# Recurrence levels kept as running products of the forget gates in a hybrid attention and recurrence decoder step

## The reference, cut to what matters

```
f = lb + (1 - lb) * sigmoid(fr);  q = silu(qr);  k = 1 - f;  v = ir
S_t = diag(f_t) S_{t-1} + k_t v_t^T          o_t = S_t^T q_t
# chunkwise: b = cumsum(log f) inside a chunk
scores[t, s] = sum_k q[t, k] * k[s, k] * exp(b[t, k] - b[s, k])   for s <= t
o = scores @ v + (q * exp(b)) @ S0
S = exp(b_last) * S0 + (k * exp(b_last - b))^T v
```

## Time and profile before

| | |
|---|---|
| time, median of 3 runs | 2099.07 us (2098.29 to 2101.21) |
| the profiled execution | 2095.78 us, of which the span of instructions is 2093.6 us |
| busy, share of the span | PE 95%, PEld 90%, DVE 57%, ACT 36%, POOL 37% |
| mean granted TensorE clock | 0.976 |
| the interleaved stage, layer 0 | 402.9 us (first `qk`) to 541.75 us (first `att_unit`) |
| the same, layer 1 | 1430.2 us to 1571.3 us |

### The profile page before, as it was taken

The page is one execution under the profiler, slowest core; times in us unless marked ns, Lnnn a source line. Parts: engine busy times, 40 slices in busy tenths (PEclk is TensorE's granted clock), DMA queues, the critical chain, the costliest instruction groups (busy, mean ns, idle before and its releaser), DMA issues.

```text
span 2093.6 us, 40399 instructions
## 1 busy us (share of the span) xinstructions
PE 1991.8 (95%) x15746; PEld 1890.4 (90%) x15746; DVE 1183.2 (57%) x2150; ACT 746.7 (36%) x1139; POOL 784.6 (37%) x452
## 2 busy tenths in 40 slices
PE   6999999988999999999999999998899999999998
PEld 6988999866799999999998889997678999999998
DVE  4577788676456442154337787886754654413531
ACT  4343232455233342222423442234632343322222
POOL 2632357210144443433465223651102434444342
PEclk9999999899899999999999999998998999999999
DMA  6232245202333232332342323541033332233322
GB/s 165 86 92 71 64 120 169 85 2 83 113 95 88 85 87 83 101 89 72 90 142 64 82 62 81 149 132 55 1 107 108 107 91 85 77 90 101 90 67 85
DMA packets 310129, 189.20 MB, mean 90 GB/s; under 512 B 15993, under 2 KB 295769, under 8 KB 308977
## 3 DMA queue, kind: packets, MB, share of 16 engines
q1 hardware_dynamic: 300368, 160.51, 27.1%
q0 software_dynamic: 4224, 16.78, 2.4%
q10 hardware_dynamic: 5408, 10.16, 1.4%
HBM read 167.47 MB, written 18.10 MB: 89 GB/s over the span
## 4 chain that ended last, share of the span: by engine, by line
PE 80%; DVE 7%; issue 4%; ACT 3%; POOL 3%; DMA 1%; PEld 0%; SPq 0%; DVEq 0%; PEldq 0%; POOLq 0%; ACTq 0%
PE acc L859 64%; PE work L1253 3%; PE work L820 2%; POOL w_lo L690 2%; PE work L1195 1%; PE work L998 1%; POOL k_sel L756 1%; DVE std L1973 1%; PE acc L1163 1%; PE work L885 1%; PE work L1288 1%; PE work L1063 1%; PE work L1101 1%; DVE mix L2621 1%; ACT w_hi L1461 1%
## 5 line engine op out<-in xcount | busy, mean ns | idle before, releaser
L690 POOL TENSOR_TENSOR w_lo<-raw,w_hi 128x1024 fp32r<-128x1024 f32 (+3 forms) x290 | 623.1, 2149 | 971.6 <-ACT w_hi L1461 967.0
L859 PE MATMUL acc<-normed,w_hi 128*128 128x268 f32 x5696 | 957.8, 290 | 3.3 <-POOL w_lo L690 1.6
L859 PEld LDWEIGHTS acc<-normed,w_hi 128*128 128x128 f32 x5696 | 801.8, 190 | 26.8 <-issue 20.0
L1461 ACT ACTIVATE w_hi<-raw 128x1024 fp32r<-128x1024 f32 (+1 forms) x286 | 289.1, 1011 | 936.6 <-PE acc L859 936.6
L859 PE MATMUL acc<-normed,w_lo 128*128 128x268 f32 x2848 | 585.0, 287 | 0.0
L859 PEld LDWEIGHTS acc<-normed,w_lo 128*128 128x128 f32 x2848 | 445.5, 189 | 0.0
L859 PE MATMUL acc<-hidden,w_hi 128*128 128x268 f32 x1408 | 231.5, 286 | 0.0
L859 PEld LDWEIGHTS acc<-hidden,w_hi 128*128 128x128 f32 x1408 | 197.0, 188 | 0.0
L859 PE MATMUL acc<-hidden,w_lo 128*128 128x268 f32 x704 | 144.2, 286 | 0.0
L2658 DVE TENSOR_TENSOR hidden<-act_f,hidden 128x536 f32 x44 | 93.3, 2121 | 50.6 <-ACT hidden L1871 50.6
L2651 DVE TENSOR_TENSOR silu<-silu,rnorm 128x536 f32<-128x536 f32 x44 | 83.4, 1895 | 59.1 <-ACT silu L1868 59.1
(11 more groups left out here) (346 smaller groups left out, 2801.2 us busy)
## 6 DMA issues: line engine op xcount, KB each, us to landing
raw<-in_w_in_dram SPq DMA_DIRECT2D x90, 512.0 KB, 3.9
raw<-in_w_gu_dram SPq DMA_DIRECT2D x88, 512.0 KB, 3.8
raw<-in_w_down_dram SPq DMA_DIRECT2D x32, 384.0 KB, 3.4
raw<-in_w_down_dram SPq DMA_DIRECT2D x32, 320.0 KB, 3.1
gate_scratch<-gate_out ACTq DMA_DIRECT2D x32, 268.0 KB, 3.0
normed<-gate_scratch SPq DMA_DIRECT2D x4, 2144.0 KB, 9.4
raw<-in_w_o_dram SPq DMA_DIRECT2D x16, 512.0 KB, 4.1
raw<-in_w_pa_dram SPq DMA_DIRECT2D x16, 256.0 KB, 3.4
```

What stands on the lines that cost most here:

```text
L690: pool.tensor_tensor(w_lo[s][:, 0:kt, :], raw[slot][:, 0:kt, :], w_hi[s][:, 0:kt, :].bitcast(f32), ALU.subtract).then_inc(lo_done, 1)
L859: mm = pe.matmul(acc[o][:, half, 0:HT], w[s][:, k, :], mov[:, part, k0 + k, half * HT:(half + 1) * HT], start=start and n == 0, stop=stop ...
L1461: act.activation(w_hi[slot % 2][:, 0:kt, :], raw[slot][:, 0:kt, :], ACT.Copy).then_inc(hi_done, 1)
```

## The change

- The logarithm, the scans, the differences, all exponentials of the recurrence and `X0` to `X2` go. q is multiplied once with f into a new buffer `XQ` (`spread(0, hp)`); k stays in `K`.
- The levels run from span 1 up to span 64, `level(i, h)`, for one head at a time, in the two 512-column halves of `work[1]` by turns. Between two levels `spread(i, hp)` multiplies, in place, the queries of each later half with the product of the gates over the earlier half, and the keys of each earlier half with that over the later one. After the seventh spread `XQ` and `K` are what the chunk steps need.
- POOL makes the products over 2, 4, ... 128 tokens in a chain of seven multiplications and a copy (`totals`, `last_decay`), ahead of the two `rest`s that stood at the stage's beginning.
- Score masks are copied for one head at a time: 28 copies of 512 columns' half in place of 14 of twice that, and four for the diagonal in place of two.
- One level per step in steps 2 to 8, chunks in steps 9 to 13, 18 steps in all. Blocks 2 and 3 change places. `qk` of block 2 stands behind the turning of the sample tokens instead of ahead.
- `s0` has memory of its own, so the first two state loads start at the stage's beginning; all four heads' sample work lies within the stage, `rank1(3)` ahead of block 15, and nothing of it between the `att_unit`s. `gate_return(0)` starts behind the turned keys of the tail.

```diff
+    SPANS = [1, 2, 4, 8, 16, 32, 64]
+    BLK = [(0, 0), (0, 1), (0, 4), (0, 2)] + [(n2, j) for j in range(3) for n2 in range(1, 4)] + [(n2, 3) for n2 in range(4)]
+    SAMPLE_OF = {11: 0, 13: 1, 15: 2, 16: 3}
+    PE_AHEAD = {1: [("diagonal", 0), ("diagonal", 1)]}
+    PE_AMID = {1: [("diagonal", 2), ("diagonal", 3)]}
+    PE_BEHIND = {1: [("v_turn", 3), ("v_turn", 4)], 2: [("level_tail", 0), ("level_tail", 1)]}
+    DVE_AHEAD = {0: ["keys"], 1: [("diagonal", 0), ("diagonal", 1)]}
+    DVE_BEHIND = {0: [("spread", 0, 0), ("spread", 0, 1)], 1: [("diagonal", 2), ("diagonal", 3)]}
+    for i in range(7):
+        tail = [("level_tail", i + 1)] if 1 <= i <= 3 else []
+        PE_AHEAD[i + 2] = [("level", i, 0), ("level", i, 1)] + tail
+        PE_AMID[i + 2] = [("level", i, 2), ("level", i, 3)]
+        DVE_AHEAD[i + 2] = [("scores", i, 0), ("scores", i, 1)] + ([("spread", i + 1, 0)] if i else [])
+        DVE_BEHIND[i + 2] = [("scores", i, 2), ("scores", i, 3)] + ([("spread", i + 1, 1), ("tail", i + 1)] if 1 <= i <= 3 else
+                                                                   [("spread", i + 1, 1)] if i else
+                                                                   [("tail", 0), ("tail", 1), ("spread", 1, 0), ("spread", 1, 1)])
+    for c in range(5):
+        PE_AMID[9 + c] = [("decayed", c)]
+        PE_BEHIND[9 + c] = [("rec_out", c), ("state", c)]
+        ACT_AHEAD[10 + c] = [("rec_out", c)]
+        DVE_AHEAD[10 + c] = [("state", c)]
...
+                for i, span in enumerate((2, 4, 8, 16, 32, 64, 128)):
+                    n = (TP if span <= 16 else 512) // span
+                    if i:
+                        wait(pool, "span_total", L, 8, i)
+                    of = (totals[i - 1] if i else B[:, 4:8, :])[:, :, 0:2 * n].rearrange("p h (b e) -> p h b e", e=2)
+                    to = totals[i][:, :, :] if i < 6 else last_decay[:, :, 0:4]
+                    pool.tensor_tensor(to, of[:, :, :, 0], of[:, :, :, 1], ALU.mult).then_inc(S["span_total"], 1)
...
-                        for h in range(4):
-                            wait(act, "forget", L, 4, h + 1)
-                            act.activation(log_f[:, h, :], B[:, 4 + h, 0:TP], ACT.Ln).then_inc(S["log_forget"], 1)
...
+                def spread(i, hp):
+                    at = slice(2 * hp, 2 * hp + 2)
+                    if i == 0:
+                        TT(XQ[:, at, :], B[:, at, 0:TP], B[:, 4 + 2 * hp:6 + 2 * hp, 0:TP], ALU.mult)\
+                            .then_inc(S["lev_ready"], 1)
+                        return
+                    span = SPANS[i - 1]
+                    w = TP if span <= 8 else 512
+                    n = w // (2 * span)
+                    if i == 1:
+                        wait_rec_filled(vec, L, ("diagonal", 2 * hp + 1))
+                        wait(vec, "tail_filled", L, 5, 2)
+                    elif i <= 4:
+                        wait(vec, "tail_filled", L, 5, i + 1)
+                    if i >= 2:
+                        wait(vec, "span_total", L, 8, i - 1)
+                    wait_rec_filled(vec, L, ("level", i - 1, 2 * hp + 1))
+                    hold(vec)
...
+                    TT(q, q, of[:, :, :, 0:1].broadcast_to((P, 2, n, span)), ALU.mult).then_inc(S["lev_ready"], 1)
+                    TT(k, k, of[:, :, :, 1:2].broadcast_to((P, 2, n, span)), ALU.mult).then_inc(S["lev_ready"], 1)
...
-                att_unit(0)
-                late_sample(2)
-                att_unit(1)
-                rank1(3)
-                att_unit(2)
-                late_sample(3)
-                att_unit(3)
+                for n in range(4):
+                    att_unit(n)
```

More of the change, by code:

```diff
@@ L1244, in diagonal @@
                                        start=True, stop=True)
-                    rec_finish(mm, ("diagonal", hp))
-                def level(lev, hp):
-                    ps, at = rec_begin(("level", lev, hp)), X[lev % 3]
-                    wait(pe, "lev_ready", L, 14, 2 * lev + 2)
-                    for m in range(8):
-                        h, c = 2 * hp + m // 4, m % 4
-                        mm = pe.matmul(ps[:, m * P:(m + 1) * P], at[:, h, c * P:(c + 1) * P], at[:, h, c * P:(c + 1) * P],
-                                       start=True, stop=True)
-                    rec_finish(mm, ("level", lev, hp))
@@ L1257, in level_tail, with level @@
-                def level_tail(lev):
-                    m = TAILS.index(lev)
-                    if m:
-                        wait(pe, "tail_drained", L, 5, m)
-                    left, right = (K, B) if lev == 7 else (X[lev % 3], X[lev % 3])
+                    rec_finish(mm, ("diagonal", h))
+                def level(i, h):
+                    ps = rec_begin(("level", i, h))
+                    wait(pe, "lev_ready", L, 30, span_ready(i, h // 2))
+                    for c in range(4):
+                        mm = pe.matmul(ps[:, c * P:(c + 1) * P], K[:, h, c * P:(c + 1) * P], XQ[:, h, c * P:(c + 1) * P],
+                                       start=True, stop=True)
+                    rec_finish(mm, ("level", i, h))
@@ L1354, in _ @@
                         rec_steps(["v_sample", "k_sample"])
+                    if block + 2 < BLOCKS:
+                        qk(block + 2)
                     if block < BLOCKS:
@@ L2402, in make_keys, with diagonal @@
                     vec.memset(state[:, :, :], 0.0).then_inc(S["state_cleared"], 1)
-                def scan(h):
+                def diagonal(h):
                     if h == 0:
-                        wait(vec, "keys", L, 4, 4)
-                    wait(vec, "log_forget", L, 4, h + 1)
-                    for r0, n in TILES:
-                        vec.tensor_tensor_scan(B[:, 4 + h, r0:r0 + n], C("ones")[:, 0:n], log_f[:, h, r0:r0 + n], 0.0,
-                                               ALU.mult, ALU.add).then_inc(S["decay_sum"], 1)
```

305 lines of the change are left out of this document (108 added, 197 removed).

## The result

The changed kernel takes 2110.25 us (median of 4 runs, 2109.69 to 2113.05); beside it the kernel before took 2098.98 (2098.29 to 2101.21). The ratio is 1.0055, with a 95% interval of 1.0037 to 1.0072. The prediction was 2081 with a range of 2071 to 2094: the time is outside it, on the other side of the kernel before. The profiled execution took 2110.55 us, span 2108.7, mean clock 0.963 where it was 0.976.

The account below looks back on a forecast made before the run. PE was taken to set the time, its idle in the levels being hidden waits for DVE. The terms sum to -8.9 us a layer, -18 for two layers, giving 2081 us against the median of 2099.07; range 2071 to 2094.

Parts of the forecast that it names:

- 1, levels: Level part: PE's 12.65 us of waits for DVE go, and 4.4 of clock loss; -17.0 us a layer.
- Steps 1 to 4: Levels, first spread, head, and the idle between head and levels, the last at -1.3 us a layer.
- 2, first spread: Start of the levels: PE stands uncovered while DVE copies and multiplies, plus hand-overs; +2.6 us a layer.
- 3, head: Head: a table load of 1.28 us goes, but block 2's `qk` no longer fills a wait; +0.4 us a layer.
- 10, POOL: Stage's beginning: POOL's product chain ends near 411, before its results are wanted; 0 us.
- rival (b): Near 410, POOL's chain and DVE's spreads block each other; 2 to 3 us a layer, 2086; 0.14, shared with partly fixed levels.
- 5 to 7: Per layer: tail's chunk gains attention beside it, -3.5 us; blocks 14 to 16 lose cover, +3.4; close idles, +4.3.
- 8, clock: Blocks 14 to 16, close and first units: idle waits bring the lower clock level; +2.2 us a layer.
- 9, samples: Sample pieces move from between the units into the stage at about the same PE price; 0 us.
- Rival (c): After block 13 PE stays at the lower clock up to the second unit; +7.5 us more, 2096, no change; chance 0.07.
- (a): Levels: DVE's copies and spreads come uncovered and pace PE; 24.5 us a layer come back, 2130; chance 0.09.
- (d): More gain at blocks 14 to 16, first spread, units and tail's chunk; -12.9 us a layer, 2073; chance 0.14.

Follow-up runs that it names:

- x3: The changed kernel with its new levels, but chunks, sample work and their drains in blocks 14 to 18 as in the kernel before; 2075.4 us, ratio 0.9888.
- x15: x3 run again: new levels, chunks and samples at their old places; 2073.4 us, ratio 0.9874.
- x4: The changed kernel with POOL's first two weight splits behind blocks 2 and 3, and the first spread-out v behind block 10's scores; 2100.5 us.
- The square: Four kernels: sample pieces out of blocks 13 to 16 or in, each with tail's chunk behind block 16 or in 13; 2083.4, 2086.3, 2098.6, 2110.3 us.
- x1: The changed kernel with head 2's sample product and head 3's rank-one update and sample product back between the attention units; 2092.9 us.
- x2: The changed kernel plus twelve unread products a layer, four in each of blocks 14, 15 and 16; 2094.8 us.
- x12: x1 with the second sample product in block 12, the tail's chunk and head 2's rank-one update behind block 16; 2083.4 us.
- x9 to x11: x3 with POOL's first two weight splits behind blocks 2 and 3, and chunks from block 14, 12 and 13 on; 2080.7, 2083.6 and 2084.5 us.

## Why the prediction was wrong, step by step

The forecast of -8.9 us a layer is made of idle time and of clock: -12.65 + 2.6 + 0.4 - 1.3 - 1.8 + 3.4 + 4.3 = -5.05 of idle, and -4.4 - 1.7 + 2.2 = -3.9 of clock. These windows, from the first `qk` to the last attention merge unit of layer 0, before and after, show what came of both:

```profile
402.94:584.54 181.60, 156.79 (x1250) 128.32 (x1250) 114.91 (x247) 84.09 (x202) 23.64 (x26) 0.89 0.23 70
```

```profile
404.11:592.75 188.64, 164.25 (x1250) 133.60 (x1250) 96.35 (x241) 62.87 (x164) 27.16 (x34) 0.81 0.22 68
```

PE idles 24.4 us instead of 24.8, so the idle time fell by 0.4 and not by 5 (in layer 1 by 1.4). And PE is busy 7.5 us longer for the same 1250 products, in layer 1 8.1, where the clock was to give 3.9 back. The clock is the larger failure, the idle time the smaller.

*1, levels (-17.0): the levels run through, but not all of the waits go.* Levels run through at 1.01 us a head; the seventh ends at 471.7, and the whole program started 1.2 us later than in the profile of before (first `qk` 404.1 against 402.9), so 470.5 against 470 forecast. In x3 and x15 the first chunk's state product begins 94.6 to 97.2 us behind the first `qk`, before it was 105.4 and 108.1: 8.2 to 13.5 a layer, 11.5 in the mean of four. Steps 1 to 4 had it at 15.3, of which 11.0 were idle time and 4.4 clock; by windows of 1 us it was 4.2 to 5.0 of idle time and 3.0 to 7.9 of clock, so about half of the levels' gain or more was clock in three of the four. Of the 12.65 us of waits that were to go, 2.15 are left in the changed kernel's levels and 4.4 in the blocks behind them; in x3 and x15 the five bare blocks wait 5.7 (17.27 of 23.00 us busy), since no level covers them any more. Missing in the sum are the keys (+1.9) and the wait at block 11 (2.0 in x3, 3.4 in the changed kernel). The second is a queueing of the kind asked about in the working, on a step where it was not counted: step 9 has the last copies and spreads of level 7 ahead of the scores, and no level left on PE to cover them.

*2, first spread (+2.6):* 2.01 measured. Right.

*3, head (+0.4): the gain came, a new loss beside it.* From the first `qk` to the sample turning it was 6.4 us and is 4.8, which the table load's 1.28 explains but for 0.3. Idle there is 2.78, not 1.7. The 1.6 gained also speak against the further 1.38 of drain that the Trainium skill gives in "ScalarE: Activation LUTs", section "What ACT_TABLE_LOAD costs"; with it, 2.7 would have gone.

*10, POOL (0): wrong in the place.* The warning was about products that meet POOL's chain. The chain ended at 408.66, ahead of the keys. What met them were the two `rest`s behind it, moved back by the chain: 3.33 us for four operations that take 1.48 when the `rest`s are elsewhere (x4). The Trainium skill, "SBUF — State Buffer", section "Who interferes with whom", also lists `tensor_scalar` among the operations that can take the port shared with GpSimd, if their operands allow it. The trace agrees with 3.33 against 1.48 us. By steps, that was rival (b) in small, and x4 showed its other half, the spread itself at 1.53 us beside a split.

*5 to 7 (-3.5 + 3.4 + 4.3):* the close was idle 4.79 us (4.3 forecast), the in-block waits 0.73 three times and 0.59 ahead of `turn(16)`, 2.8 in all (3.4 forecast). Both right. Of the tail's 3.5 the idle 1.8 went; the 1.7 of clock did not, the chunk now stands in the low stretch. The unit phase is shorter by 6.3 us in layer 0 (556.24 to 592.75; before, 541.75 to 584.54) and by 4.6 in layer 1, 5.5 forecast.

*8, clock (+2.2): here it failed.* This term priced idle time ("1.5 inside, and 0.7 more than before in the units") as what pulls the clock down. By the windows, 25.56 us of work at 0.52 and 9.13 at 0.50 lose 25.56 x 0.48 + 9.13 x 0.50 = 16.8 us of a layer, and the first units up to 559.5 another 1.6; before, 30.32 us at 0.99 and 10.00 at 0.51 lost 5.2 (the windows at the end of this section). That is 13.2 more. It is nearer to 12 if a row at the lower level takes 1.97 / 1.09 = 1.8 times as long and not twice. With the -1.7 of step 5, which is clock too, the prediction had +0.5 for this stretch. It is **+12**. *9, samples (0)*, is the same error: the pieces' own PE price was moved about unchanged, but not what they do to the blocks around them. The square gives 7.5 a layer for that alone, and 7 to 8 of clock. Rival (c) named the outcome with "clock near 0.5 from block 14 on" and was given 0.07; its size, 7.5 on top of the 2.2, was nearer and still short of 12, and "unit or sample pieces stand between them" stood there as an argument against it. The runs show the reverse: with the sample pieces in blocks 15 and 16 the clock stayed low to 559, and without them (x1) to 531. Why the stretch ends where it does stays open: in x2 and x4 it ended at 530 and 529 with the pieces in place.

With 12 in place of 0.5, the keys' 1.9 and block 11's 3.4, the sum is -8.9 + 11.5 + 1.9 + 3.4 = +7.9 a layer. The profiled executions have +7.0 and +6.7, the medians 11.3 / 2 = 5.6.

*The other rivals.* (a) did not happen: no level but the first waits for a spread. (d) did not either.

The windows of the kernel before over the stretch of step 8, where all its chunks stood:

```profile
505.00:538.00 33.00, 30.32 (x242) 24.71 (x242) 17.86 (x53) 12.08 (x27) 1.37 (x3) 0.99 0.46 143
538.00:548.00 10.00, 10.00 (x45) 9.63 (x45) 3.03 (x8) 0.64 (x2) 0.00 (x0) 0.51 0.18 52
```

## What to carry to other kernels

Split a large change into what it speeds up and what it moves: here the new levels alone beat both kernels (2073 to 2075 us), and the reordering done with them cost more than they gave. When matmul work is moved, price the pieces with few columns or few rows not by their own time but by the clock of the work around them, and keep them away from a stretch that has nothing large beside it; between large products they cost little more than their own time (three pieces between the merge units made them 4.6 to 6.3 us longer). And when a group of operations leaves a queue, ask who is pushed back behind what took its place: here POOL's splits, into DVE's keys.

## What the runs showed of the hardware

- PE at 95% busy got a mean clock of 0.52 for 27 us, in a low stretch of 44 us on end, while at 74 and 75% busy it held the upper level for 13 us (x12) and for 23 us (x15). By these rows busy time alone does not say which level is granted. What stood in the low stretch and not in the others was one-column, 8-row and 16-row products.
- Twelve added products of no use in each layer (3 us at full speed) made the kernel 15.5 us faster; its mean clock went from 0.962 to 0.971.
- A DVE product of two SBUF tensors took 1.53 us beside a POOL operation of 1.26 (x4), and 0.71 without; four `tensor_scalar` operations took 3.33 us beside two of POOL's, and 1.48 without.
- The pieces act together: 15 and 3 us alone, 27 in common, of which the chunk's 3 alone are idle time. An edit that touched only the head and block 11 (x4) turned the low stretch of 44 us behind block 13 into two of 10 and 17, and x9 to x11 spread over 13 to 18 us from run to run, with the clock. What decides where a low stretch ends is not settled by these runs.
